# Encoder step on one core: the second group's projections are divided four before and 23 inside the first expert phase

## The reference, cut to what matters

```python
h   = RMSNorm(x)
z   = h @ w_in           # 6664 columns: queries, keys, values of two attentions, 8 forget logits, 2 x 1024 gates
o_A = DiffAttn(q_A, k_A, v_A)      # 8 heads x 2 maps, chunk-causal mask, relative bias, RMSNorm per head
o_B = FoX(q_B, k_B, v_B, logf)     # 8 heads, causal, decay by the cumulated log of the forget gate
x   = x + (sigmoid(g_A) * (o_A @ w_pa) + sigmoid(g_B) * (o_B @ w_pb)) @ w_o
x   = x + PEER(RMSNorm(x))         # below
y   = RMSNorm_final(x)

# PEER, per token: 8 heads, each picks 16 of 128 x 128 experts by two sets of 128 keys
s1, i1 = top_k(q1 @ keys1, 16);  s2, i2 = top_k(q2 @ keys2, 16)
top, pos = top_k(s1[:, None] + s2[None, :], 16);  e = expert index of pos
out = sum_k softmax(top)_k * gelu(u[e_k] . xb) * v[e_k]
```

## Time and profile before

| | |
|---|---|
| time, median of 3 runs | 2407.07 us (2404.95 to 2410.33) |
| time of the profiled execution | 2407.02 us |
| its span | 2405.2 us |
| TensorE busy in the span | 1894.5 us (79%) |
| VectorE busy | 1509.2 us (63%) |
| GpSimd busy | 739.2 us (31%) |
| ScalarE busy | 594.6 us (25%) |
| moved from HBM and to it | 765 MB, 318 GB/s in the mean |
| dots (line 1584), 544 | 1220 ns each |
| adds of v on VectorE (line 1609), 222 | 1285 ns each |

### The profile page before, as it was taken

The page is one execution under the profiler, slowest core; times in us unless marked ns, Lnnn a source line. Parts: engine busy times, 40 slices in busy tenths (PEclk is TensorE's granted clock), DMA queues, the critical chain, the costliest instruction groups (busy, mean ns, idle before and its releaser), DMA issues. The chain is left out here.

```text
span 2405.2 us, 22936 instructions
## 1 busy us (share of the span) xinstructions
PE 1894.5 (79%) x7392; PEld 1118.4 (47%) x7392; DVE 1509.2 (63%) x3470; ACT 594.6 (25%) x1631; POOL 739.2 (31%) x697
## 2 busy tenths in 40 slices
PE   7889897899886876896787778857776898787665
PEld 6855674457544642343662234445532344563210
DVE  0021208787665478766668868656697776659956
ACT  3231011311241121442022234301222343013211
POOL 0000000444323123333334524332344433334533
PEclk9988999999987887987898889879988788899888
DMA  7741654999879887779999987699999677999887
GB/s 247 274 145 54 211 200 141 420 421 394 317 296 342 305 311 273 290 297 348 403 398 404 353 322 304 275 399 402 421 381 381 259 292 261 411 412 388 343 325 304
DMA packets 139303, 765.00 MB, mean 318 GB/s; under 512 B 18608, under 2 KB 42464, under 8 KB 52016
## 3 DMA queue, kind: packets, MB, share of 16 engines
q0 software_dynamic: 78336, 570.46, 60.1%
q1 hardware_dynamic: 27632, 161.42, 18.0%
q10 hardware_dynamic: 33216, 31.67, 4.0%
HBM read 744.77 MB, written 18.30 MB: 317 GB/s over the span
## 5 line engine op out<-in xcount | busy, mean ns | idle before, releaser
L646 POOL DMA_INDIRECT ring<-in_uv,stage x544 | 672.8, 1237 | 1208.5 <-issue 401.5
L1261 PE MATMUL acc<-ring,diag 128*128 128x512 f32 (+1 forms) x1268 | 693.0, 697 | 250.3 <-DVE diag L1595 127.4
L1584 DVE CUSTOM_DVE_ANT_0 ring<-ring,xb 128x1024 f32<-128x1024 f32 x544 | 648.2, 1220 | 133.3 <-DMA ring<-in_uv,stage 114.1
L1261 PEld LDWEIGHTS acc<-ring,diag 128*128 128x128 f32 (+1 forms) x1268 | 261.1, 217 | 635.0 <-issue 289.9
L920 ACT ACTIVATE gel<-dots 128x1 f32<-128x1 f32 x544 | 101.4, 200 | 891.7 <-DVE dots L1584 881.9
L1609 DVE SCALAR_TENSOR_TENSOR vsum<-ring,coefd,vsum 128x1024 f32<-128x1024 f32 x222 | 285.4, 1285 | 8.9 <-DVE coefd L1602 0.8
L1034 PE MATMUL pz<-F,wbuf 128*128 128x416 f32 (+1 forms) x656 | 240.5, 526 | 25.0 <-ACT F L781 19.6
L664 POOL COPY stage<-idx 128x4 int32<-128x4 int32 x136 | 63.7, 468 | 431.8 <-DVE gw L1540 411.4
L1034 PEld LDWEIGHTS pz<-F,wbuf 128*128 128x128 f32 (+1 forms) x656 | 125.0, 193 | 136.5 <-issue 136.5
L1602 DVE TENSOR_SCALAR coefd<-gel,gw 128x1 f32<-128x1 f32 x227 | 47.6, 210 | 148.8 <-ACT gel L920 148.2
L1595 DVE TENSOR_SCALAR diag<-ident,gel,gw 128x128 f32<-128x128 f32 x159 | 55.9, 361 | 96.1 <-ACT gel L920 93.9
(11 more groups left out here) (312 smaller groups left out, 2159.9 us busy)
## 6 DMA issues: line engine op xcount, KB each, us to landing
wbuf<-in_w_z SPq DMA_DIRECT2D x52, 1024.0 KB
wbuf<-in_w_q SPq DMA_DIRECT2D x40, 1024.0 KB
wbuf<-in_w_pa SPq DMA_DIRECT2D x20, 1024.0 KB
wbuf<-in_w_o SPq DMA_DIRECT2D x20, 1024.0 KB
wbuf<-in_w_pb SPq DMA_DIRECT2D x20, 512.0 KB
ring<-in_uv,stage POOLq DMA_INDIRECT x544
zT<-F ACTq DMA_DIRECT2D x28, 208.0 KB, 5.3
wbuf<-in_w_sk SPq DMA_DIRECT2D x5, 1024.0 KB
```

The source lines that it names most:

```text
L646: pool.indirect_dma_start(out=ring[:, slot, :], out_offset=None, in_=d["uv"], in_offset=bass.IndirectOffsetOnAxis(ap=stage[:, a, k:k + 1], ...
L1261: last = nc.tensor.matmul(acc[0:nq, c * 512:(c + 1) * 512], diag[:, parity, 0:nq], ring[:, slot, D + c * 512:D + (c + 1) * 512], start=Fal ...
L1584: nc.vector.tensor_tensor_reduce(out=u, in0=u, in1=xb[:, t % 2, :], scale=1.0, scalar=0.0, op0=ALU.mult, op1=ALU.add, accum_out=dots[:, sl ...
```

## The change

The constant `LATER` goes from 17 to 23, so 4 instead of 10 pieces of group 1 stand in the front of tile 0 and 23 in phase 0. The weight of a piece in the dealing goes from 12 to 10. The query load of tile 1 moves on ScalarE from the end of the front of tile 0 to behind piece 8 of group 1, since the last query piece is now inside phase 0.

```diff
--- before.py
+++ after.py
@@ -75,7 +75,7 @@
 CHUNKS = len(PROJ)
 
 GROUPS = [(0,), (1, 2, 3, 4)]
-LATER = 17
+LATER = 23
 ZSTAGES = 4
 FINISHED = 4
 
@@ -127,7 +127,7 @@
 
     what, i, p = event
     if what == "project":
-        return 12.0
+        return 10.0
     if p == 0:
         return 12.0 if i == TILES - 1 else 4.0
     if ATTEND <= p < NORM_O:
@@ -786,6 +786,8 @@
                         act.wait_ge(z_stored, z + 1)
                         k0 = z_first[kind] + f.start
                         act.dma_start(zT_t[:, k0:k0 + len(unit), group_cols(g)], dst).then_inc(z_saved[b], 16)
+                if g and i == Q_CHUNKS + 1:
+                    load_q(1)
                 if i == 3:
                     act.wait_ge(flog_ready, g + 1)
                     act.dma_start(d["o_lfT"][:, group_cols(g)], flog_g[0:8, 0:n]).then_inc(logf_saved, 16)
@@ -901,8 +903,6 @@
                 elif p == PIECES - 1:
                     act.wait_ge(g_shift, t + 1)
                     nc.scalar.activation(fa(t).cand[0:nq, :, 1, :], fa(t).cand[0:nq, :, 0, :], ACT.Exp).then_inc(g_exp, 1)
-                    if t == 0:
-                        load_q(1)
 
             def pack_sample():
```

## The result

The changed kernel took 2429.71 us in the median of 5 runs (2423.76 to 2439.57), the kernel before 2407.07 us. The ratio is 1.0103, 95% interval 1.0075 to 1.0132, so the change made the kernel slower by about 1% (18 to 32 us). Forecast were 2425 us and a range of 2411 to 2440 us. The profiled execution of the changed kernel is the longest of the five, 2439.57 us with a span of 2437.8 us.

What follows compares the result with a forecast made beforehand. TensorE was taken to set the pace of the first expert phase, with DMA close behind in its first half. 70.3 - 30.3 - 10.9 - 1.3 - 9.7 = +18.1 us on 2407.07 gave 2425 us, range 2411 to 2440 us.

Steps and rivals of the forecast that it cites:

- 16 wide pieces instead of 10 (F): Projection restart to last value piece: six more wide pieces at 11.72 us each, nothing hiding them, +70.3 us.
- attention of tile 0 (B): First attention matmul of tile 0 to first transpose of its outputs: fewer pieces, less slow-clock cost, -30.3 us.
- before the norm (C): First output transpose to end of tile 0's scores: VectorE's wait for the norm-weight spread goes, -10.9 us.
- routing (D): End of tile 0's scores to gate weights: two of three pieces removed, worth nothing as VectorE sets the end, 0.
- restart (E): Gate weights to projection restart: a query copy replaces a gate sigmoid, so a table load falls away, -1.3 us.
- half blocks: up to attention (G): Last value piece to tile 1's first attention matmul: two half blocks left there instead of three, -3.7 us.
- half blocks: attention of tile 1 (H): Tile 1's first attention matmul to first output transpose: nine half blocks instead of ten, -3.3 us.
- its turn to its scores (I): First transpose of tile 1's attention outputs to the end of its scores: no change, 0.
- half blocks: routing of tile 1 (J): End of tile 1's scores to its seed: one half block leaves the routing, two dots fewer on VectorE, -2.7 us.
- The DMA rival: First expert phase: DMA sets the pace, six pieces cost only their bytes, 21 us; kernel at 2386 us; chance 0.03.
- The two routing pieces: Beside tile 0's routing: their removal gains nothing, yet they are paid at full price in the expert phase, 11.72 us each.
- The clock in packed attention: Tile 0's attention: steps without wide pieces run at the lower clock, taking 7.9 us off a 38.2 us saving.

Runs made afterwards that it cites:

- e4: The changed kernel run again with no edit, for a second trace: 2429.09 us, ratio 1.0108 to the kernel before.
- e7: The kernel before with only an eighth of each weight load of the 17 pieces in phase 0: 2404.68 us, ratio 0.9998.
- e3: The kernel before with only the new weight of 10 per piece in the dealing instead of 12: 2406.22 us, ratio 1.0009.
- e9: The changed kernel with weight 12 and tile 1's query load behind piece 16 instead of 8: 2425.22 us, ratio 1.0089 to the kernel before.
- e8: The changed kernel with phase 0's wide pieces multiplied over four of eight slices of the model width: 2412.22 us, ratio 1.0017 to the kernel before.
- e1: The changed kernel with two of its 23 phase 0 pieces put back beside tile 0's routing: 2411.35 us, ratio 1.0025 to the kernel before.
- e5: The kernel before with one of four pieces in tile 0's attention moved beside the routing: 2397.53 us, ratio 0.9973.
- e6: The kernel before with two attention pieces of tile 0 moved to the routing, the last behind its end in the order: 2393.60 us, ratio 0.9949.
- e2: The changed kernel with the old weight of 12 per piece in the dealing: 2433.59 us, ratio 1.0118 to the kernel before.
- e10: The changed kernel with piece 1 moved from tile 0's attention to the routing: 2424.13 us, ratio 1.0075 to the kernel before.

## Why the prediction was right

Against the terms of its sum, by the trace of the changed kernel (and e4):

```
term                                    forecast   changed    e4
16 wide pieces instead of 10 (F)          +70.3      +71.6   +71.8
attention of tile 0 (B)                   -30.3      -30.0   -31.9
before the norm (C)                       -10.9       -8.3    -7.5
routing (D)                                 0          0.0     0.0
restart (E)                                -1.3       -1.7    -1.7
half blocks: up to attention (G)           -3.7       -4.0    -4.0
half blocks: attention of tile 1 (H)       -3.3       -1.7    -4.5
its turn to its scores (I)                  0         +1.9    +0.7
half blocks: routing of tile 1 (J)         -2.7       -3.7     0.0
sum                                       +18.1      +24.2   +22.8
```

The forecast of 2425 us stands against 2429.71, and the seed of tile 1 came 22.7 and 22.0 us later, where some 18 were named. The mechanism of the two large parts, F and the routing, is shown by the runs; the smaller terms agree less well than the table looks.

- *TensorE sets the pace of the first expert phase.* Right. F stayed at 205 us when the DMA rate fell (e7) and when fewer gathers stood in it (e3), and at 277 us with more (e9). The DMA rival, with its forecast of 2386 us, falls. But with half of TensorE's work gone from the wide pieces only 20.6 us go (e8), so 11.7 us is the price of a piece only as long as TensorE is this slow. The Trainium skill, page "Perfetto Trace Analysis", section "Identifying the Most-Contended Engine", would judge TensorE by weight-load busy time and by MFU (the share of its peak arithmetic rate that it reaches), and not by matmul busy time. Weight-load busy time, 60.7 of 119 us, would have misled here; MFU was not worked out.
- *The two routing pieces are the core.* Shown by e1: putting just these two back shortens B to J by 15.3 to 16.7 us (845.6 and 844.2 against 828.9), of the 22.8 to 24.2 us that the change added, and takes 18 us off the median. In e5 and e6 even a fourth piece beside the routing left D at 54.4 us.
- *The clock in packed attention.* Right in kind: 0.50 from 154.4 to 179 us with TensorE busy 24.60 of 24.60 us. The size is in part luck. B is 30.0 and 31.9 us shorter than in the one trace of the kernel before, but that trace has a long B (94.0 us); against e3 and e7, with 90.4 us for the same program, the change saves 26.4 to 28.4 us, where the sum has 30.3. The Trainium skill, page "TensorE: Matmul & The Clock Gate", section "HAM oscillation — how this bites in real kernels", names idle gaps as what costs the clock. The first fall does not speak against that, since 2.98 us without work stand ahead of it. The second fall does: from the wide piece at 179.02 to 206 us there is no gap of more than 0.2 us, and yet the clock went from 1.00 to 0.50 at about 194.5.
- *Before the norm* the table shows 3 us too little, and this too is the one trace of before. C is 118.4 us in it and 120.9 and 121.0 in e3 and e7. The kept piece between the transposes took 11.34 us there, but 13.11 in the changed kernel and 13.03 in e3 and e7, whose TensorE order up to there is that of the kernel before. The row of e3:

```profile
237.02 13.03 PE L1034 MATMUL pz<-F,wbuf 128*128 128x416 f32 x32
```

  Against e3 and e7, C is 9.9 to 10.9 us shorter, which is the forecast. B and C together are 37 to 39 us shorter by every pair of traces, where the sum has 41.2; the term that was too large by 2 to 4 us is the attention's. Its clock cost may be what is missing, since the steps behind the kept piece run at 0.50 from 194.7 us on and the sum had 1 us for them; that was not taken apart.
- *The first wide piece after the restart* took 14.11 us instead of 12.91. The longer idle time is not the reason: in e1 it took 14.11 us after only 17.71 us of idle time. The cause stays open.
- *Half blocks.* The first part (G) came as forecast. For H, I and J the two traces of one program differ by up to 4 us each; together they are -3.5 and -3.8 us, where I had -6.0. The prediction had no clock term there, and one is missing: the attention of tile 1 starts at a granted clock of 0.52 and 0.50 instead of 1.00 for 17 us, and reaches its eighth group of bias matmuls 6.5 and 6.9 us later. All the traces whose half blocks are dealt otherwise than before show such slow first matmuls (1.22 us instead of 0.70), in e3 too, where nothing else is changed; the four with the dealing of before (before, e5, e6, e7) do not. Against that, 3.3 us for a half block in H look too low: e1 and the changed kernel, both with the slow start, differ by two half blocks and 9.8 to 12.6 us there, which makes an estimate of 4.9 to 6.3 each; a part of it may be clock, 0.76 in e1 against 0.80 and 0.83. The two errors go in opposite directions, so that H came near its forecast is in part luck. How much each one weighs was not taken apart.
- *The signs named.* Gate weights at 375.1 us (named: 374; counted from the first attention matmul they are 3 us late), last value piece at 663.9 (661), idle beside the routing 41.4 us (40 or more). One was off: the DMA share of the wide pieces fell only to 0.97, not well under 1.01; the rate of 384 GB/s and the wait of 1.3 us for rows show the slack better.
- *Moved load, SP, GpSimd: 0.* Right for the changed kernel, though in e2 the load made F 5.5 us longer.

## What to carry to other kernels

Before moving work out of a stage, ask of each piece what it hides behind there: here two of six pieces stood beside a routing that lasts 54.4 us with or without them, and moved into a stretch where TensorE had no gap they cost 11.7 us each. When two resources both look full, the waits tell which one the chain ends at, and cutting the traffic of the other (e7) settles it. Before a difference between two traces is explained, a second trace of the same program should be at hand: B differs by 3.6 us between traces of the kernel before's order, as much as some of the terms in question. The way to gain was the opposite move: filling TensorE's idle time beside the routing with pieces from the attention gave 0.5% (e6).

## What the runs showed of the hardware that was not expected

- The clock fell to half in a stretch without a gap of more than 0.2 us: after the wide piece at 179.02 us of the changed kernel the granted clock was 1.00 from 191.4 to 194.2 us and 0.50 from 194.7 to 206, with narrow matmuls (128 columns and less) and transposes and TensorE busy 11.09 of 11.30 us. At the lower level it also stayed with TensorE busy 24.60 of 24.60 us, and in e10 at 0.50 or 0.51 over some 39 us.
- Issuing one 208 KB write took 11.40 us instead of 0.33 when it stood 5.6 us behind the start of a strided read of 768 KB on the same queue, while gathers were running (e2). It is not the distance alone: 9.3 us behind it took 0.33 us (changed kernel), 11.7 us behind it took 7.29 us (e8).
- Traces of the same program differ by up to 11 us in the 150 us ahead of the attention (144.0 to 155.3 us over the kernels, whose instructions up to there do not differ) and by 11 us over the last four phases (1445.6 and 1434.4 us).
